# A two-layer decoder: second layer's rgb tile fetched by GpSimd into another region, first weight unit in its own transfer, gathers and stores read the index column directly

## The reference

```python
for i in range(2):
    m = short_conv_mixer(x, ...) if i == 0 else chunked_sgu_mixer(x, ...)
    x = layer_norm(ALPHA * x + m, ln_mix_g[i], ln_mix_b[i])
    logits = x @ router_w                       # scores = sigmoid(logits)
    # best of 4 groups, its best 2 experts, gates normalised to sum 1
    f = sum(gates[:, e:e+1] * ((silu(x @ w_gate[e]) * (x @ w_up[e])) @ w_down[e]) for e in range(16))
    x = layer_norm(ALPHA * x + f, ln_ffn_g[i], ln_ffn_b[i])
```

## Time and profile before

| What | Value |
|---|---|
| median of 3 runs | 1196.63 us (1195.35 to 1196.99) |
| profiled execution, its own time | 1197.66 us |
| its span | 1196.0 us |
| PE matmul busy | 1089.8 us, 91% of the span |
| DVE, ACT, POOL busy | 825.2, 634.4, 159.6 us |
| mean granted clock | 0.964 of full speed |
| HBM traffic | 251 GB/s over the span |

### The profile page before, as it was taken

How to read it: one execution, slowest core, us unless ns; L and a number is a source line. 1 busy time by engine, 2 the same in 40 slices (tenths; PEclk the granted TensorE clock), 3 DMA queues, 4 the chain that set the end, 5 groups by cost and what they waited for, 6 DMA issues and landing times.

```text
span 1196.0 us, 15224 instructions
## 1 busy us (share of the span) xinstructions
PE 1089.8 (91%) x5326; PEld 856.3 (72%) x5326; DVE 825.2 (69%) x1010; ACT 634.4 (53%) x743; POOL 159.6 (13%) x154
## 2 busy tenths in 40 slices
PE   6999999899999999919999999599989999999960
PEld 5888888477777777718887888488657777777740
DVE  5454466679889989874534546136768889999947
ACT  4322333368878888721435332113347878888931
POOL 1000000103322222500000000000002121122112
PEclk9999999999999999959999999799999999999985
DMA  8224323689999999872313212420579999999933
GB/s 312 96 88 194 140 89 124 210 335 400 395 383 381 383 377 386 340 296 95 141 46 137 100 71 79 168 71 36 184 265 375 398 389 379 374 388 380 397 118 139
DMA packets 49871, 288.81 MB, mean 241 GB/s; under 512 B 9080, under 2 KB 9240, under 8 KB 20112
## 3 DMA queue, kind: packets, MB, share of 16 engines
q1 hardware_dynamic: 36816, 255.87, 55.5%
q0 software_dynamic: 8080, 16.76, 4.1%
q10 hardware_dynamic: 4912, 15.33, 3.5%
HBM read 277.07 MB, written 23.07 MB: 251 GB/s over the span
## 4 chain that ended last, share of the span: by engine, by line
PE 84%; DMA 6%; DVE 6%; ACT 1%; issue 1%; SPq 0%; ACTq 0%; DVEq 0%
PE ps L466 25%; PE ps L468 25%; PE ps L467 25%; DMA raw_more<-in_w_moe 3%; PE ps L1765 2%; DMA Y<-y_rows 1%; DVE hot L498 1%; PE ps L1923 1%; PE ps L1671 1%; DVE lo L462 1%; PE ps L1823 1%; PE ps L1841 1%; DMA rgb<-in_ln_par 1%; PE ps L1689 1%; PE ps L1790 1%
## 5 line engine op out<-in xcount | busy, mean ns | idle before, releaser
L462 DVE TENSOR_TENSOR lo<-raw,hi 128x1024 fp32r<-128x1024 f32 x312 | 368.3, 1222 | 120.8 <-ACT hi L451 118.1
L451 ACT ACTIVATE hi<-raw 128x1024 fp32r<-128x1024 f32 x312 | 315.8, 1054 | 162.9 <-PE ps L468 97.0
L466 PE MATMUL ps<-hi,xgT_hi 128*112 128x512 f32 x480 | 190.7, 397 | 0.4 <-DVE xgT_lo L1376 0.4
L468 PE MATMUL ps<-hi,xgT_lo 128*112 128x512 f32 x480 | 188.3, 392 | 0.0
L467 PE MATMUL ps<-lo,xgT_hi 128*112 128x512 f32 x480 | 187.6, 391 | 0.0
L462 DVE TENSOR_TENSOR lo<-raw_more,hi 128x1024 fp32r<-128x1024 f32 x128 | 153.3, 1220 | 26.8 <-ACT hi L451 24.4
L451 ACT ACTIVATE hi<-raw_more 128x1024 fp32r<-128x1024 f32 x128 | 132.1, 1056 | 58.6 <-DMA raw_more<-in_w_moe 45.6
L466 PE MATMUL ps<-xT_hi,hi 128*128 128x512 f32 x320 | 127.4, 398 | 13.0 <-DVE lo L462 11.4
L467 PE MATMUL ps<-xT_lo,hi 128*128 128x512 f32 x320 | 125.3, 392 | 0.0
L468 PE MATMUL ps<-xT_hi,lo 128*128 128x512 f32 x320 | 125.1, 391 | 0.0
L849 POOL COPY idx_col<-idx 128x1 int32<-128x1 int32 x30 | 17.0, 567 | 688.7 <-DVE idx L506 513.9
(11 more groups left out here) (193 smaller groups left out, 1515.4 us busy)
## 6 DMA issues: line engine op xcount, KB each, us to landing
raw<-in_w_moe SPq DMA_DIRECT2D x128, 1024.0 KB
raw_more<-in_w_moe SPq DMA_DIRECT2D x64, 1024.0 KB
raw<-in_w_dense SPq DMA_DIRECT2D x40, 1024.0 KB
Y<-y_rows SPq DMA_DIRECT2D x16, 512.0 KB, 7.7
x_rows<-X ACTq DMA_DIRECT2D x8, 512.0 KB, 2.6
xT_raw<-in_x_t SPq DMA_DIRECT2D x4, 512.0 KB, 9.0
X<-in_x SPq DMA_DIRECT2D x1, 2048.0 KB, 10.0
mix_par<-in_ln_par ACTq DMA_DIRECT2D x4, 512.0 KB, 8.4
```

Of the source, the lines that this page charges most:

```text
L451: nc.scalar.activation(hi[:, s, :], flat(raw_units(n)), ACT.Copy).then_inc(hi_ready, 1)
L462: eng.tensor_tensor(lo[:, s, :], flat(raw_units(n)), hi[:, s, :], ALU.subtract).then_inc(lo_ready, 1)
L466: nc.tensor.matmul(out_, a_hi, b_hi, start=first, stop=False)
L468: return nc.tensor.matmul(out_, a_lo, b_hi, start=False, stop=last)
```

## The change

Four edits to order and place; the arithmetic is the same.

1. `rgb[1]` is issued by POOL as soon as `g_ready` has reached 14, no longer by ACT at the end of the gated tiles, and with `r_prod[1]`, `r_sum[1]` and `ones_g` it moves to 56 to 59 KB, which is V[12] and V[13]. DVE does `router_prod(1)` one unit earlier and `router_weights(1)` one unit earlier.
2. Unit 0 comes in a transfer of its own with its own semaphore, right behind the first quarter of x; unit 1 follows behind the fourth quarter.
3. ACT issues its six small transfers behind the rounding of the four quarters and of unit 0, no longer ahead of them.
4. Gathers and stores take the column of `idx` or `odx` itself; the copies L849 and L858 go, and with the first the wait for `xrow_out[0]`.

```diff
@@ -219,9 +219,9 @@
         x0 = place("x0", [P, KD, P], F32, 56 * KB)
         h0 = place("h0", [P, KF, P], F32, 28 * KB)
         rw2 = [place("rw2_0", [P, KD, E], F32, 71 * KB), None]
-        rgb = [place(f"rgb{l}", [2 * KD, P], F32, o) for l, o in ((0, 72 * KB), (1, 60 * KB))]
-        r_prod = [place(f"r_prod{l}", [P, 2, KD, E], F32, o) for l, o in ((0, 73 * KB), (1, 61 * KB))]
-        r_sum = [place(f"r_sum{l}", [P, 2, E], F32, o) for l, o in ((0, 75 * KB), (1, 62 * KB))]
+        rgb = [place(f"rgb{l}", [2 * KD, P], F32, o) for l, o in ((0, 72 * KB), (1, 56 * KB))]
+        r_prod = [place(f"r_prod{l}", [P, 2, KD, E], F32, o) for l, o in ((0, 73 * KB), (1, 57 * KB))]
+        r_sum = [place(f"r_sum{l}", [P, 2, E], F32, o) for l, o in ((0, 75 * KB), (1, 58 * KB))]
         xg = place("xg", [P, 2, D], F32, 8 * KB)
         xgT_hi = place("xgT_hi", [P, KD, P], F32R, 16 * KB)
         xgT_lo = place("xgT_lo", [P, KD, P], F32R, 20 * KB)
@@ -240,7 +240,7 @@
 
         ident = place("ident", [P, P], F32)
         ones_f = place("ones_f", [P, P], F32, 68 * KB + 256)
-        ones_g = place("ones_g", [P, P], F32, 60 * KB + 512)
+        ones_g = place("ones_g", [P, P], F32, 58 * KB + 512)
         ones_b = place("ones_b", [P, P], BF16)
         tri = place("tri", [P, P], BF16)
         iota_s = place("iota_s", [P, P], BF16)
@@ -337,6 +337,7 @@
             return ctx.enter_context(nc.semaphore(name))
 
         raw_in = [sem(f"raw_in{s}") for s in range((RING + MORE) // 2)]
+        unit0_in = sem("unit0_in")
         hi_ready = sem("hi_ready")
         lo_ready = sem("lo_ready")
         unit_used = sem("unit_used")
@@ -444,7 +445,9 @@
         def split_hi(act, n, step=0, i=0):
 
             s = slot_of(n)
-            if n % 2 == 0:
+            if is_zero(n):
+                act.wait_ge(unit0_in, 16)
+            elif n % 2 == 0 or n == 1:
                 act.wait_ge(raw_in[raw_slot(n) // 2], at(PAIRS, n, step, i) * 16)
             if BEFORE[n] is not None:
                 act.wait_ge(unit_used, at(INDEX, BEFORE[n], step, i) + 1)
@@ -525,7 +528,7 @@
 
             return pool.indirect_dma_start(
                 out=xg[0:T, half, :], out_offset=None, in_=x_rows[:, :],
-                in_offset=bass.IndirectOffsetOnAxis(ap=idx_col[0:T, col:col + 1], axis=0),
+                in_offset=bass.IndirectOffsetOnAxis(ap=col, axis=0),
                 bounds_check=S - 1, oob_is_err=False)
 
         def gathers(layer, c):
@@ -587,7 +590,7 @@
                     pool.reg_mov(spare, used)
                     used = spare
                 pool.wait_ge(xrow_out[0], 16 * (layer + 1))
-                gather(pool, 0, 0).then_inc(o.xg, 16)
+                gather(pool, 0, idx_col[0:T, 0:1]).then_inc(o.xg, 16)
                 for k in range(EP):
                     if k >= 2:
                         pool.wait_ge(o.used, q * EP + (k - 1))
@@ -738,7 +741,8 @@
                 sp.dma_start(xT_raw[:, 2 * c:2 * c + 2, :].rearrange("p k s -> p (k s)"), x_t[c, :, :]) \
                   .then_inc(xt_in[c], 16)
                 if c == 0:
-                    load_pair(0, w_dense0[0, :, :])
+                    sp.dma_start(raw[:, 0, :], w_dense0[0, :, 0:UN]).then_inc(unit0_in, 16)
+            sp.dma_start(raw[:, 1, :], w_dense0[0, :, UN:2 * UN]).then_inc(raw_in[0], 16)
             for m in (1, 2):
                 load_pair(2 * m, w_dense0[m, :, :])
             with sp.Fori(0, 3) as i:
@@ -845,19 +849,14 @@
                     pool.wait_ge(xgT_ready, n - 1)
                     if gathers(layer, c) > 1:
                         pool.wait_ge(xg_in[b], 16 * (gathers(layer, c) - 1))
-                src = idx[:, e:e + 1] if isinstance(e, int) else idx[:, bass.ds(e, 1)]
-                chain.step(nc.gpsimd.tensor_copy(idx_col[:, b:b + 1], src))
-                pool.wait_ge(xrow_out[0], 16 * (layer + 1))
-                gather(pool, b, b).then_inc(xg_in[b], 16)
+                gather(pool, b, idx[0:T, e:e + 1]).then_inc(xg_in[b], 16)
 
             def add_out(layer, c, i=0):
 
                 e, b, n = plus(c, i), c % 2, plus(c + E * layer, i)
                 pool.wait_ge(y_copied, n + 1)
-                src = odx[:, e:e + 1] if isinstance(e, int) else odx[:, bass.ds(e, 1)]
-                chain.step(nc.gpsimd.tensor_copy(out_col[:, b:b + 1], src))
                 pool.wait_ge(slot_gate_ready, layer + 1)
-                scatter(pool, layer, y[0:T, b, :], out_col[0:T, b:b + 1]).then_inc(y_out[b], 16)
+                scatter(pool, layer, y[0:T, b, :], odx[0:T, e:e + 1]).then_inc(y_out[b], 16)
 
             def experts(layer):
                 for t in range(NT):
@@ -884,6 +883,8 @@
             for t in range(NT):
                 pool.wait_ge(second_in[t], 16)
             pool.dma_start(bsb[:, :, :].rearrange("p h i -> p (h i)"), b_s.partition_broadcast(P)).then_inc(bs_in, 16)
+            pool.wait_ge(g_ready, 14)
+            pool.dma_start(rgb[1][:, :], ln_par[1, 0, :, :].rearrange("g (k p) -> (g k) p", p=P)).then_inc(rgb_in[1], 16)
             experts(1)
             overflow_pool(pool, 1, spare)
             for t in range(NT - 1):
@@ -903,15 +904,15 @@
 
                 preloads.step(nc.scalar.activation(warm[:, :], eps[:, :], func))
 
-            for o, i_ in ((rw[:, :, :], router_w), (rbias[:, :], router_bias.partition_broadcast(P)),
-                          (cw[:, :, :], conv_w), (vg[:, :], v_gain), (vb[:, :], v_bias)):
-                act.dma_start(o, i_).then_inc(small_in, 16)
-            act.dma_start(rgb[0][:, :], ln_par[0, 0, :, :].rearrange("g (k p) -> (g k) p", p=P)).then_inc(rgb_in[0], 16)
             for c in range(4):
                 act.wait_ge(xt_in[c], 16)
                 copy(xT_hi[:, 2 * c:2 * c + 2, :], xT_raw[:, 2 * c:2 * c + 2, :]).then_inc(xt_hi, 1)
                 if c == 0:
                     split_hi(act, 0)
+            for o, i_ in ((rw[:, :, :], router_w), (rbias[:, :], router_bias.partition_broadcast(P)),
+                          (cw[:, :, :], conv_w), (vg[:, :], v_gain), (vb[:, :], v_bias)):
+                act.dma_start(o, i_).then_inc(small_in, 16)
+            act.dma_start(rgb[0][:, :], ln_par[0, 0, :, :].rearrange("g (k p) -> (g k) p", p=P)).then_inc(rgb_in[0], 16)
             for n in range(1, CRING):
                 split_hi(act, n)
             act.dma_start(ws_sum[:, :, :], w_s).then_inc(ws_in, 16)
@@ -1153,7 +1154,6 @@
             act.wait_ge(g_lo_ready, NC)
             act.dma_start(X[:, :, :], x_mid.ap().rearrange("(t p) d -> p t d", p=P)).then_inc(x_back, 16)
             params(1, 0, mix_par[1])
-            act.dma_start(rgb[1][:, :], ln_par[1, 0, :, :].rearrange("g (k p) -> (g k) p", p=P)).then_inc(rgb_in[1], 16)
             for n in range(12, 16):
                 split_hi(act, SO0 + n)
 
@@ -1543,11 +1543,11 @@
                     own_lo(SO0 + 8 + (j - NC // 2) // 2)
             dve.wait_ge(ws_copied, 2)
             nc.vector.memset(ones_g[:, :], 1.0).then_inc(ones_ready, 1)
+            router_prod(1)
             own_lo(SO0 + 12)
-            router_prod(1)
             own_lo(SO0 + 13)
+            router_weights(1)
             own_lo(SO0 + 14)
-            router_weights(1)
             own_lo(SO0 + 15)
             dve.wait_ge(x_back, 16)
             dve.wait_ge(unit_used, SO0 + 8)
```

## The result

The changed kernel took 1177.28 us (median of 4 runs, 1175.66 to 1178.65), the kernel before in the same comparison 1196.81 us (1195.35 to 1198.94). The ratio is 0.9838, 95% interval 0.9824 to 0.9852: 17.7 to 21.1 us faster, 19.5 by the medians. 1177.5 was predicted. The profiled execution took 1176.74 us, its span 1175.1 us.

What follows compares the result with a forecast made beforehand. PE bounds the experts, busy for all of 100 us, so only its standstills, some 106 us, can be won. Middle 16.1 + start 2.6 + end 0.5 = 19.2 us, giving a median of 1177.5 us, range 1175.3 to 1180.6.

Steps and rivals of the forecast that it cites:

- Middle, 16.1 us: Around PE's wait for rgb[1] in layer 1: the edit wins 13.7 us of wait and 2.4 of lost clock.
- covers: Layer 1's router: rgb[1] lands at about 745, PE needs it at 753.8; X has 8.8 us before its first use.
- The direct POOL transfer: rgb[1] issued by POOL: 1.2 us issue plus 9.3 to landing, middle values from gathers and a store.
- POOL held up by DVE: At rgb[1]'s transfer: POOL might write no descriptors before 742.5; landing at 752.6, same gain, cover only 1.2 us.
- Start, 2.6 us: First matmuls: PE starts earlier with unit 0 alone and small transfers later; 2.6 us, range 1.2 to 3.4.
- The working by bytes moved: Start: at 409 GB/s from 4 us, unit 0 lands at 6.3 us and PE starts at 8.7, not 11.41.
- The feared waits for unit 1 and for the mask: First 30 us: unit 1 just in time or up to 1.4 us late; POOL's mask fits by 0.5 us.
- Experts and end, 0.5 us: Removed copies: nothing in the experts; last store 1.0 us sooner, worth 0 to 1.0 us at the end, 0.5 taken.
- (a): Rival at the start: small issues, unit 1 or mask leave 0 to 1 us of gain; 1179.5 us, chance 0.10.
- (b): Rival in layer 1's router: late rgb[1] or X makes a new wait, 5 us given back; 1182.5, chance 0.05.
- (c): Rival in the experts: indirect DMAs reading the wide index tile issue slower, POOL becomes the bound; 1250 us, chance 0.02.
- (d): Rival across the kernel: more than summed, through a shorter half-clock stretch or earlier-settling first stores; 1175 us, chance 0.03.

Runs made afterwards that it cites:

- the eightfold dose: The changed kernel with eight copies of the index column on POOL added ahead of each gather and each store: 1182.97 us, ratio 0.9885.

## Why the prediction was right, point by point

- **Middle, 16.1 us: right.** At the place itself the trace gives 19.62 us from 753.53 to the fourteenth matmul before and 3.60 after (750.59 to 754.19), 16.0. From the last expert turn of layer 0 to L1605 the two profiles differ by 15.3 us, and edit 1 alone gave 14.6 (12.3 to 16.9). Both are single draws: over all profiles that stage takes 300.7 to 301.7 us in the five kernels with the long wait (mean 301.4) and 284.8 to 286.6 in the seven profiles with none (mean 285.6), 15.9 us apart, and the profile before has the shortest of the five. That nothing else would hold PE is shown: covers of 17 and 12 us where 8.6 and 8.8 were counted. The direct POOL transfer was over-sized, 2.0 us to landing against 9.3. In the seven profiles that issue it from POOL it took 2.0 to 2.2 us, with the engines at a share of 0.74 in one (731 to 734 us) and 0.53 in another (edit 1 alone, 736 to 739.5 us). The gather was the wrong neighbour: it moves 0.46 MB and this transfer 8 KB.
- **POOL held up by DVE: not at this transfer, but elsewhere.** POOL's issue at 731.99 took 0.52 us amid DVE's work, 0.52 in all seven profiles. The stores of the experts tell another story. POOL and DVE near the end of layer 0's experts, before and then after:

```profile
475.51 8.46 POOL L537 DMA_INDIRECT y_rows<-y,out_col  x1 [0.81 <-POOL out_col L858]
474.58 0.61 DVE L1387 TENSOR_TENSOR hT_lo<-ps,hT_hi 128x448 fp32r<-128x448 f32 x1
475.11 4.62 DVE L462 TENSOR_TENSOR lo<-raw,hi 128x1024 fp32r<-128x1024 f32 x4
479.65 3.48 DVE L462 TENSOR_TENSOR lo<-raw_more,hi 128x1024 fp32r<-128x1024 f32 x3
483.06 0.68 DVE L1383 TENSOR_TENSOR hid<-sgate,ps 112x512 f32<-112x512 f32 x1
```

```profile
470.31 1.52 POOL L540 DMA_INDIRECT y_rows<-y,odx  x1 [16.50 <-ACT y L1012]
470.92 0.62 DVE L1387 TENSOR_TENSOR hT_lo<-ps,hT_hi 128x448 fp32r<-128x448 f32 x1
```

Before, the copy makes the store start just behind `hT_lo`, and it ends at 483.97, 0.91 us behind the start of the next DVE instruction that reads `ps`. After, the store starts ahead of `hT_lo` and ends at 471.83, again 0.91 us behind its start. All six kernels with one copy have such a store near the end of layer 0, of 8.46 or 8.47 us and with its end 0.91 to 0.93 us behind the start of `hid`; of the six profiles without copies none has a store above 1.6. So POOL seems to be held there for as long as DVE works out `lo` without a break. The 8.46 us that the prediction took as the upper end of an issue are such a wait. In the turns they cost nothing that can be seen: edit 1 alone has two of them, and no turn above 17.66 us.
- **Start, 2.6 us: right**, 2.54 at L1589. The working by bytes moved was off by 0.2 us at unit 0. Its split holds: the size of the pair was counted at 1.3 us and gave 1.26 alone, and the small transfers gave 1.27 on top of it (1.92 alone). The feared waits for unit 1 and for the mask did not come; the mask had 1.8 us in hand and not 0.5, because `ws_sum` was issued at 16.85 instead of 18.11.
- **Experts and end, 0.5 us: a term mis-sized on both sides.** The last store came 0.25 us sooner, not 1.0, and stands 0.79 us behind `y`, not 0.2, since the 0.79 us of wait come with the indirect DMA. In the experts the prediction counted nothing. Against that the whole of edit 4 measured 1.3 and 1.25 us, twice not clear of zero. If it is real, its place is open: the end shows 0.1 to 0.3 us, and in the turns the means over the profiles speak for the copies and the eightfold dose against them.
- **Rivals.** (a), the start eaten: fell. (b), a new wait: fell. (c), POOL as the bound because of the wide column: fell, gathers have a median of 0.99 us against 1.20 and stores 1.37 against 1.68. (d), 1175, lies below every median of the whole change (1176.85 to 1178.17).

```profile
L529 POOL DMA_INDIRECT xg<-x_rows,idx x30: 980/987/1975, 211.6 to 1071.1; - x30
L540 POOL DMA_INDIRECT y_rows<-y,odx x32: 933/1372/1539, 255.4 to 1135.8; - x32
```

The profiled pair differs by 20.9 us and the medians by 19.5: the execution profiled before had the longest turns of the 13 profiles. The forecast's 19.2 met the medians, and the terms that it missed were small. That it met them within 0.3 us is partly luck: the whole change gave 19.5, 20.0 and 18.7 us on three occasions. What the prediction's signs had wrong besides is small: X is first used 25.0 us behind the transpose and not 22.5.

## What to carry to other kernels

When a small transfer holds an engine, look first at what is issued ahead of it in the same queue: moving 8 KB ahead of 3 MB won all but 2 of the 16 us, and the earlier moment, with its new region and another engine, only the rest. At the start of a kernel look at the size of the packets in flight and not only at the bytes. Before crediting an edit with a microsecond that two profiles show, compare the same stage between executions that don't contain the edit.

## What was not expected of the hardware

- After 1.9 us in which PE waited, the granted clock stayed 1.00 and the pace 0.23 us; after 13.7 us it was 0.52 for 5.3 us, at 2.4 us of cost in the execution before.
- The slow pace at the start (0.43 us a matmul) lasted 3.5 us in one execution of the changed kernel and 5.95 in another. It is read from the pace alone: the column of the granted clock says 1.00 there.
- A plain DMA issued by POOL landed in 2.0 to 2.2 us (seven profiles), one of the same bytes issued by ACT in 1.8 (one). The Trainium skill ("DMA: Bandwidth & Descriptors", section "SWDGE vs HWDGE vs iDMA") calls the hardware's setup faster than POOL's; the times to landing fit that, 0.2 to 0.4 us apart, at different moments and with the setup not shown by itself.
- With one copy ahead of it a store of POOL took 8.46 us where it took 1.52 without: it started 0.3 us behind the end of a DVE instruction that reads `ps`, and not ahead of its start, and then lasted until the next such instruction.
